# Early groups loaded a group ahead, tables on another queue, 29 units ahead of the gate matrix

## The reference

```
p  = x @ w_in                                    # q, k, v of mixers A and B, two gates
yA = attention over own chunk + 8 previous, relative-position bias per head
yB = windowed grouped attention, ALiBi penalty, a learned sink per head
h  = LN1(a*x + (sig(gA)*(yA@w_a) + sig(gB)*(yB@w_b)) @ w_out)
q  = h @ w_query  -> 8 heads x 2 halves; s1 = q1 . sub_keys_1; s2 = q2 . sub_keys_2
v1,i1 = top16(s1); v2,i2 = top16(s2); sc,ci = top16(v1 + v2)   # 16 experts per head
gate = softmax(sc); experts = e1*128 + e2        # of 128*128 experts
y  = LN2(a*h + sum over experts of gate * gelu(u[expert].h) * v[expert])
```

## Time and profile before

| | |
|---|---|
| median of 3 runs | 4519.07 us (4515.66 to 4525.55) |
| the profiled execution | 4518.42 us, span 4516.6 us |
| busy: PE, PEld, DVE, ACT, POOL | 90%, 87%, 62%, 37%, 66% of the span |
| mean granted TensorE clock | 0.947 of full speed |
| DMA | 1341.35 MB, mean 297 GB/s |

### The profile page before, as it was taken

One profiled execution on the slowest core, in us unless ns is written; L12 is line 12 of the kernel. 1 busy time (PEld: TensorE's weight loads), 2 busy tenths in 40 slices (PEclk: granted clock), 3 DMA queues, 4 the chain that ended last, 5 costly groups with the idle time before them and its releaser, 6 DMA issues. The chain is left out here.

```text
span 4516.6 us, 71733 instructions
## 1 busy us (share of the span) xinstructions
PE 4082.8 (90%) x26789; PEld 3927.0 (87%) x26789; DVE 2798.5 (62%) x4041; ACT 1666.0 (37%) x2837; POOL 2982.2 (66%) x1624
## 2 busy tenths in 40 slices
PE   7999999999998998997999789899999998787867
PEld 7988889999977877996999788899999998787867
DVE  2112322377566788875987677666776676767775
ACT  3433444443233444323335455433333333222223
POOL 6843457675754554774567466698888887676754
PEclk8988999999999998998999899999999999898989
DMA  8755446554998898995358799999999999898973
GB/s 257 226 162 154 129 140 206 160 171 139 418 359 343 344 365 327 399 389 203 117 163 318 274 325 336 336 406 416 417 416 415 415 416 385 340 379 320 383 306 102
DMA packets 366152, 1341.35 MB, mean 297 GB/s; under 512 B 35968, under 2 KB 148480, under 8 KB 280448
## 3 DMA queue, kind: packets, MB, share of 16 engines
q0 software_dynamic: 93760, 682.66, 37.2%
q1 hardware_dynamic: 141696, 510.20, 33.0%
q10 hardware_dynamic: 130496, 145.99, 9.3%
HBM read 1277.73 MB, written 65.80 MB: 297 GB/s over the span
## 5 line engine op out<-in xcount | busy, mean ns | idle before, releaser
L480 POOL TENSOR_TENSOR w_lo<-w_raw,w_hi 128x1024 fp32r<-128x1024 f32 x968 | 2345.3, 2425 | 1192.1 <-ACT w_hi L942 1170.1
L942 ACT ACTIVATE w_hi<-w_raw 128x1024 fp32r<-128x1024 f32 x968 | 1018.6, 1056 | 1315.0 <-DMA w_raw<-in_wstream 636.0
L1461 DVE CUSTOM_DVE_ANT_0 rows<-rows,banks 128x2048 f32<-128x2048 f32 x320 | 728.4, 2281 | 285.3 <-DMA rows<-in_u_rows,idx_all 284.5
L1464 DVE SCALAR_TENSOR_TENSOR banks<-rows,act_n,banks 128x2048 f32<-128x2048 f32 x320 | 752.2, 2350 | 211.9 <-DMA rows<-in_v_rows,idx_all 208.9
L879 PE MATMUL banks<-weighted,w_hi 128*128 128x320 f32 x3072 | 699.8, 317 | 92.7 <-DVE work L1856 66.8
L824 PE MATMUL banks<-mv_hi,w_hi 128*128 128x320 f32 x2048 | 654.1, 319 | 91.2 <-ACT work L1308 54.7
L545 PE MATMUL banks<-mv,w_hi 128*128 128x256 f32 x3648 | 697.9, 293 | 35.3 <-POOL w_lo L480 27.9
L545 PE MATMUL banks<-mv_hi,w_hi 128*128 128x384 f32 x1824 | 635.4, 348 | 49.6 <-ACTq L1196 21.5
L824 PE MATMUL banks<-mv_lo,w_hi 128*128 128x320 f32 x2048 | 641.9, 313 | 0.0
L824 PE MATMUL banks<-mv_hi,w_lo 128*128 128x320 f32 x2048 | 641.8, 313 | 0.0
L545 PEld LDWEIGHTS banks<-mv,w_hi 128*128 128x128 f32 x3648 | 593.3, 200 | 45.4 <-issue 28.3
(11 more groups left out here) (179 smaller groups left out, 5430.2 us busy)
## 6 DMA issues: line engine op xcount, KB each, us to landing
w_raw<-in_wstream SPq DMA_DIRECT2D x968, 512.0 KB, 5.6
gate_matrix<-work ACTq DMA_DIRECT2D x20, 1024.0 KB
work<-gate_matrix ACTq DMA_DIRECT2D x16, 1280.0 KB, 10.8
early_act<-work ACTq DMA_DIRECT2D x64, 160.0 KB, 6.1
work<-early_act ACTq DMA_DIRECT2D x64, 160.0 KB
out_p<-work ACTq DMA_DIRECT2D x34, 192.0 KB, 3.6
gate_scratch<-work ACTq DMA_DIRECT2D x32, 192.0 KB, 7.4
work<-gate_scratch ACTq DMA_DIRECT2D x16, 384.0 KB, 10.6
```

The costliest lines, as they stand in the source:

```text
L480: pool.tensor_tensor(w_lo[s][:, part], raw[s][:, part], w_hi[s][:, part].bitcast(f32), ALU.subtract) \
L942: act.activation(w_hi[s][:, HALVES[h]], raw[s][:, HALVES[h]], ACT.Copy).then_inc(hi_late, 1)
L1461: ins = dve.tensor_tensor_reduce(rows, rows, nat, 1.0, 0.0, ALU.mult, ALU.add, weight)
L1464: ins = dve.scalar_tensor_tensor(nat, rows, weight, nat, ALU.mult, ALU.add)
```

## The change

Five parts. `TAIL` goes from 19 to 29, so 35 units run beside the gate matrix and `QUAD_STEPS` becomes 7. `RATES` changes for four ranges. In the gate loop ScalarE calls `gate_rows(q + 2)` after the unit events. The tables are issued by SP, one after each unit of units 2 to 15 (the constants in four parts, 14 DMAs in all), for which the qkv loop is written out. And the early groups' gates and activations get two buffers each with a semaphore per buffer (`early_in`), `load_early(i)` issues both together, one group earlier than before; regular groups keep `G4`.

```
@@ -22,6 +22,7 @@
 SCALE = HD ** -0.5
 NEG = -1e30
 BIG = 3e38
+TABLES = 6 + 8
 PICKS = PH * TOPK
 
 G3 = 64
@@ -35,7 +36,7 @@
 GBLK = ND // GT
 GATE_Q = ND // 4
 AHEAD = 4
-TAIL = 19
+TAIL = 29
 GATE_UNITS = N_EARLY - TAIL
 QUAD_STEPS = GATE_UNITS * KT_N // GATE_Q
 ROWS = 4
@@ -84,8 +85,8 @@
         ITEMS.append(("h", _b, 0))
 FIRST_OF = {(z, b): ITEMS.index((z, b, 0)) for z, b, p in ITEMS if p == 0}
 GATHER_AT = AT["b4"] + 12
-RATES = ((GATHER_AT, AT_GATE[1], 2.3), (AT_GATE[1] + 1, AT_PROJ[1], 4.2), (AT_PROJ[1], AT_OUT[1], 2.2),
-         (AT_OUT[1], AT_QUERY[1], 2.0), (AT_EARLY + GEXP_AT, AT_EARLY + TAIL, 1.9), (AT_EARLY + TAIL, AT_LATE, 1.6))
+RATES = ((GATHER_AT, AT_GATE[1], 2.3), (AT_GATE[1] + 1, AT_PROJ[1], 4.2), (AT_PROJ[1], AT_OUT[1], 2.4),
+         (AT_OUT[1], AT_QUERY[1], 2.2), (AT_EARLY + GEXP_AT, AT_EARLY + TAIL, 2.2), (AT_EARLY + TAIL, AT_LATE, 1.2))
 
 
 
@@ -374,7 +375,8 @@
         sq_l = [W2[:, 6080 + ND * s:6080 + ND * s + ND] for s in range(2)]
         g_buf = [R[:, 5120 + 2048 * w:5120 + 2048 * w + 2048].rearrange("p (e t) -> p e t", t=GT) for w in range(2)]
         G4 = R[:, 5120:5120 + EG * ND].rearrange("p (b e t) -> p b e t", b=GBLK, e=EG)
-        act_in_t = [R[:, 7680 + ND * e:7680 + ND * e + ND] for e in range(EG)]
+        act_in_t = [[a[:, at + ND * e:at + ND * e + ND] for e in range(EG)] for a, at in ((R, 7680), (x_raw, 3072))]
+        G4_early = [a[:, 0:EG * ND].rearrange("p (b e t) -> p b e t", b=GBLK, e=EG) for a in (W2[:, 5632:], R[:, 5120:])]
 
         banks = ctx.enter_context(nc.psum_tensor("banks", [P, 8, 512], f32))
         nat = banks[:, 4:8, :].rearrange("p b c -> p (b c)")
@@ -426,7 +428,6 @@
         oh_ready, oh_gated, g_full, g_evac = sem("oh_ready"), sem("oh_gated"), sem("g_full"), sem("g_evac")
         g_stored = [sem(f"g_stored{w}") for w in range(2)]
         act_stored = [sem(f"act_stored{s}") for s in range(2)]
-        act_in = sem("act_in")
 
         rows_in = [sem(f"rows_in{s}") for s in range(ROWS)]
         rows_used, nat_ready, act_n_ready, act_n_gelu = (
@@ -434,6 +435,7 @@
         hb_taken, hb_stored, n_var, n_std, n_ready, n_stored, half_copied, acc_high = (
             sem(n) for n in ("hb_taken", "hb_stored", "n_var", "n_std", "n_ready", "n_stored", "half_copied", "acc_high"))
 
+        early_in = [sem(f"early_in{z}") for z in range(2)]
         g4_in, gelu_done, w_prod, wwh_done, w_ready, out_evac = (
             sem(n) for n in ("g4_in", "gelu_done", "w_prod", "wwh_done", "w_ready", "out_evac"))
         dve_own, dve_apart, pool_apart = sem("dve_own"), sem("dve_apart"), sem("pool_apart")
@@ -453,8 +455,33 @@
                     sp.wait_ge(mv_in[1], 16)
                 for h in range(2):
                     sp.dma_start(raw[s][:, HALVES[h]], wstream[:, s, HALVES[h]]).then_inc(raw_half[s][h], 16)
+
+            def table(dst, src):
+                sp.dma_start(dst, src).then_inc(tab_done, 16)
+
+            def bias_table(n):
+
+                rt, n_r = rext.tensor, rext.shape[1]
+                if n == 0:
+                    table(bp_a[:, 64:P, :], bass.AP(rt, 63, [[n_r, 16], [-1, 64], [1, 512]]))
+                elif n == 1:
+                    table(bp_a[:, 0:64, 0:448], bass.AP(rt, 127, [[n_r, 16], [-1, 64], [1, 448]]))
+                elif n < 6:
+                    h = slice(4 * n - 8, 4 * n - 4)
+                    table(bp_a[h, 0:64, 448:512], negs[h])
+                elif n < TABLES:
+                    b = DEC_T * (n - 6)
+                    table(bs_a[:, b:b + DEC_T, :], bass.AP(rt, 383, [[n_r, 16], [-1, 16], [1, 144]]))
+
             for name, unit, count in SEGMENTS:
-                first = 1 if name == "qkv" else 0
+                if name == "qkv":
+                    for i in range(1, count // 2):
+                        for s in range(2):
+                            for h in range(2):
+                                load(2 * i + (AT[name] + s), 2 * i + (unit + s), s, h)
+                            bias_table(2 * i - 2 + s)
+                    continue
+                first = 0
                 if count == 2:
                     for s in range(2):
                         for h in range(2):
@@ -1221,12 +1248,6 @@
                 load(subkt[:, :], subk, const_in)
                 load(sinkt[:, :], sinks, const_in)
                 load(lnt[:, :], lnp, const_in)
-                rt, n_r = rext.tensor, rext.shape[1]
-                load(bp_a[:, 64:P, :], bass.AP(rt, 63, [[n_r, 16], [-1, 64], [1, 512]]), tab_done)
-                load(bp_a[:, 0:64, 0:448], bass.AP(rt, 127, [[n_r, 16], [-1, 64], [1, 448]]), tab_done)
-                load(bp_a[:, 0:64, 448:512], negs, tab_done)
-                for b in range(DEC_B):
-                    load(bs_a[:, DEC_T * b:DEC_T * b + DEC_T, :], bass.AP(rt, 383, [[n_r, 16], [-1, 16], [1, 144]]), tab_done)
 
             for i in range(N_QKV):
                 if i == 2:
@@ -1234,7 +1255,7 @@
                 if i == 6:
                     load_constants()
                 if i == 26:
-                    act.wait_ge(tab_done, 16 * (3 + DEC_B))
+                    act.wait_ge(tab_done, 16 * TABLES)
                     first_loads(0)
                 qkv_slot(AT["qkv"] + i, i, 0)
                 if 4 <= i < 4 + KT_N:
@@ -1357,27 +1378,27 @@
                     act.wait_ge(g_stored[w], 16 * (blk // 2))
                 act.activation(g_buf[w][:, :, 4 * qq:4 * qq + 4],
                                banks[:, 2 + q % 2, :].rearrange("p (t e) -> p e t", t=4), ACT.Copy).then_inc(g_evac, 1)
-                if q + 2 < GATE_Q:
-                    gate_rows(q + 2)
                 for u, h in quad_events(q):
                     if h == 0:
                         split_high(AT_EARLY + TAIL + u + 2, 0)
                     else:
                         early_activation(TAIL + u)
+                if q + 2 < GATE_Q:
+                    gate_rows(q + 2)
                 if qq == 3:
                     act.wait_ge(g_evac, q + 1)
                     act.dma_start(G_s[:, :, blk, :, :].rearrange("g p e t -> p g (e t)"),
                                   g_buf[w].rearrange("p (g e) t -> p g (e t)", e=EG)).then_inc(g_stored[w], 16)
 
 
-            def load_gates(q):
-
-                g = (q + EARLY) % GROUPS
-                load(G4.rearrange("p b e t -> p (b e t)"), G_s[g].rearrange("p b e t -> p (b e t)"), g4_in)
-
-            def load_acts(i):
+            def load_gates(r):
+
+                load(G4.rearrange("p b e t -> p (b e t)"), G_s[EARLY + r].rearrange("p b e t -> p (b e t)"), g4_in)
+
+            def load_early(i):
+                load(G4_early[i % 2].rearrange("p b e t -> p (b e t)"), G_s[i].rearrange("p b e t -> p (b e t)"), early_in[i % 2])
                 for e in range(EG):
-                    load(act_in_t[e], a_s[EG * i + e], act_in)
+                    load(act_in_t[i % 2][e], a_s[EG * i + e], early_in[i % 2])
 
             def high_part(z, q, e, src):
                 act.wait_ge(w_prod, EG * q + e + 1)
@@ -1402,15 +1423,16 @@
                 i = q + 1 - REGULAR
                 if 0 <= i < EARLY:
                     for e in PREP[v]:
-                        high_part(1 - i % 2, q + 1, e, act_in_t[e])
+                        high_part(1 - i % 2, q + 1, e, act_in_t[i % 2][e])
                 split_high(n + 2, 1)
-                if v == 0 and q + 1 < GROUPS:
-                    act.wait_ge(w_prod, EG * (q + 1))
-                    load_gates(q + 1)
-                    if 0 <= i < EARLY:
-                        if i:
-                            act.wait_ge(w_ready, EG * (q + 1))
-                        load_acts(i)
+                if v == 0:
+                    if q + 1 < REGULAR:
+                        act.wait_ge(w_prod, EG * (q + 1))
+                        load_gates(q + 1)
+                    nxt = q + 2 - REGULAR
+                    if 0 <= nxt < EARLY:
+                        act.wait_ge(w_ready, EG * (q + 1))
+                        load_early(nxt)
 
             for w in range(2):
                 act.wait_ge(g_stored[w], 16 * (GBLK // 2))
@@ -1821,10 +1843,10 @@
 
             dve.sem_inc(out_evac, 4)
 
-            def product(act, e):
+            def product(act, gates, e):
 
                 a3 = act.rearrange("p (b t) -> p b t", b=GBLK)
-                dve.tensor_tensor(a3, a3, G4[:, :, e, :], ALU.mult).then_inc(w_prod, 1)
+                dve.tensor_tensor(a3, a3, gates[:, :, e, :], ALU.mult).then_inc(w_prod, 1)
 
             def low_part(z, q, e, src):
                 dve.wait_ge(wwh_done, EG * q + e + 1)
@@ -1847,7 +1869,7 @@
                 if e == 0:
                     dve.wait_ge(g4_in, 16 * r + 16)
                 dve.wait_ge(gelu_done, N_EARLY + EG * r + e + 1)
-                product(bank_of(e), e)
+                product(bank_of(e), G4, e)
                 if e == EG - 1:
                     low_part(0, r, e, bank_of(e))
 
@@ -1866,12 +1888,11 @@
                 i = q + 1 - REGULAR
```

(32 more changed lines are left out.)

43 lines of the change are left out of this document (21 added, 22 removed).

## The result

The changed kernel takes 4362.2 us (median; 4356.1 to 4363.4, 4 runs), the kernel before 4520.0 us beside it (4515.7 to 4525.6): ratio 0.9639, 95% interval 0.9624 to 0.9655. The gain is 158 us; 86 were forecast (4432 us). The profiled execution spans 4361.4 us, before 4516.6; the mean granted clock is 0.966, before 0.947.

The account below looks back on a forecast made before the run. Bytes were taken to pace the full-DMA stages, with the tables, gate matrix and early groups not full. Terms: 68 - 15 + 24 + 9 = 86 us off 4518.4, so 4432 us; range 4358 to 4474.

Parts of the forecast that it names:

- rival (c): Whole kernel: tables 15, projections 8 lost, units and gate matrix 60, early groups 83; 150 us gained, 4368 us; chance 0.20.
- 24 forecast: Early units and gate matrix: 108 + 153 + 340 + 4 = 605 us against 629, gain 24; ends +74 and -3.
- Three engines within 7% of each other never overlap wholly: Gate matrix with 35 units: TensorE 312, DMA 303, VectorE 291 us, so 340 taken, between 329 and 367.
- Rival (d): Gate matrix: each quad paced by its own chain, not its GEMM; 144 us more than forecast, 4576 us; chance 0.05.
- not added: Gate matrix: ScalarE serving units first removes TensorE's 54.7 us gelu wait, most of it already inside the 24 us.
- 68 forecast: Early groups loaded a group ahead: 537 us becomes 469, between DMA floors of 453 and 478; ends 83 and 45.
- rival (b): Early groups: VectorE paces them at 72 us a group, gain 33 instead of 68, 4467 us; chance 0.15.
- (e): Early groups: loading ahead brings nothing, seven periods of 76.7 us again, 4500 us; chance 0.07.
- The first wait ... nothing: Early groups' wait at 3846: its 2.6 MB only move one group forward into a full stage, so no gain.
- -15 forecast: Two projections: 3 more gathers in each, 3.15 MB at full DMA, 15.8 us; 15 lost, ends 0 and 16.
- 9 forecast: Tables on SP's queue: TensorE's 15.2 us wait goes, 6.3 us exposed, gain 9; ends 15 and -8.
- The half of 12.5 us that was to stay exposed: Tables on SP's queue: the large two cost 12.5 us of landing time, 6.3 of it taken as exposed.

Follow-up runs that it names:

- both edits taken back: Changed kernel with TAIL 19, the old rates and ScalarE's old order back, loads ahead and tables kept: 4423.6 us, ratio 0.9744 to the kernel before.
- the runs that take the six steps out: Changed kernel, projections at 2.2 and 2.0 gather steps per unit: steps to attention 4380.8 us, to units 14-28 4372.3; TAIL 19 4367.2, with old order too 4423.6.
- 3.8 steps: Changed kernel with 3.8 gather steps per unit beside the second half's attention instead of 4.2: 4378.5 us, ratio 0.9679 to the kernel before.

## Why the prediction was right or wrong

The time fell 70 us below the forecast, inside the range, and within 6 us of rival (c), "everything closes", 4368 us. Most of the mechanisms were the forecast's; three terms were mis-sized. By the table the kernel gained 69 us more than the sum: 45 in the early units and the gate matrix, 26 in the early groups and 12 by the tables, less 12 in the regular groups and 2 before the early units.

**Early units and gate matrix: 24 forecast, 69 measured.** The step that failed is "Three engines within 7% of each other never overlap wholly", with which 340 us were taken between 329 and 367 although TensorE's own floor was 312. The upper end was also worked out wrong: without the norm's 60 us the old stage has TensorE at 382 of 426 us, not of 450, so 0.90 and 348 us. And the old stage's share of TensorE, 0.86 over all of it, was no general loss of overlap. It was for the most part one coupling, the 174.4 and 54.7 us of the earlier trace rows: ScalarE held the gelu behind a late one-hot row. That was seen, and called "most of" the 24. With the coupling gone TensorE runs at 0.98, and the stage (first mask to last early gelu, 2502.0 to 2825.0) takes 323 us, 17 less than taken. Units 14 to 28, forecast at 153 us (131 by bytes and a hole of 22 for the norm), took about 132: DMA was idle in 8% of 140 us, 11 us, and only 3% from 2380 on, so most of the hole overlapped with gathers. The rest, some 10 us, is the passage from the last early to the first regular gelu, which the forecast did not price: 19.7 us before, 9.4 after; it is 19.0 with both edits taken back, 9.7 to 10.7 with one, and 9.4 to 13.6 in kernels with both and the same deal. (24 + 17 + 21 + 10 = 72, 3 too many: 2 are the 6 us from unit 28's gelu to the first mask, for which 4 were taken, and 1 is the old stage's end, 2890 for 2888.5.) Rival (d), 5.3 us or more per quad, was wrong: 323 / 80 = 4.0.

**The order, "not added" to the 24.** Right in effect, for a reason that the forecast did not have: beside 29 units it is worth nothing, and alone 51 us. One cure for one coupling was enough.

**Early groups: 68 forecast, 94 in the last stretch less some 7 to 8 in the regular groups.** For the period of 66 to 68 us the forecast was right: 65.8, DMA at 1.01, VectorE at 352 of 395 us, so not rival (b) at 72, nor (e) at 76.7. Six periods give 57.8 of the 93.8 us. The mis-sized part is the end. The forecast let seven periods shrink by one measure, DMA's floor, and gave the last group nothing. But from the last gate load on DMA is at 0.65, no floor: there the waits removed (33.8 us before, two of up to 17.1) come back whole, 246.7 - 211.1 = 35.6 us; TensorE's clock rose there too, from 0.87 to 0.94. "The first wait ... nothing" was too kind: 2.6 MB moved into a full stage cost what they cost everywhere, 2.6 / 0.41 = 6.3 us, and the regular gelus took 7.3 us more with this part alone and 7.7 less without it. The rest of their 12.4 us lies in the spread: in kernels with the same number of gathers there they took 907.4 to 912.5 us with the loads ahead, and 900.1 to 904.8 without, but 912.6 in the one with the order alone, which is left open.

The 358 GB/s of the Trainium skill ("DMA: Bandwidth & Descriptors", section "Where 436 GB/s comes from") did not bind here either: the changed kernel's trace has 410 GB/s, held for 395 us by weights, gathers, gates and activations together.

**Projections: -15 forecast, -12.8 measured**, 9.7 us per unit of the first as forecast (145.6 / 15); the runs that take the six steps out give 10.6 to 14.7 back. By bytes, as worked out. The 3.7 us of the attention before them, which no part of the change touches, lie within its spread (522.4 to 534.0 us in kernels with the same deal).

**Tables: 9 forecast, 22 alone and 18 in company.** The stretch of 57 to 80 us, called not full, was full: DMA 1.00 in the earlier trace rows. The half of 12.5 us that was to stay exposed is not seen: DMA is at 0.86 from 57 to 80 us where it was 1.00, TensorE fully busy there. The 14 DMAs lie between weights that are two units ahead, and TensorE's waits up to 100 us name none of them. The term that failed is the 6.3 us taken as exposed. The ends given, -8 to 15, did not hold the gain. TensorE's first 130 us, before and after:

```profile
0.00:130.00 130.00, 98.70 (x768) 98.06 (x769) 36.28 (x31) 51.40 (x79) 85.25 (x39) 0.91 0.79 250
0.00:130.00 130.00, 115.24 (x912) 114.24 (x913) 49.01 (x34) 60.40 (x91) 98.50 (x45) 1.00 0.85 277
```

It is ahead by 144 matmuls, which at 169 in 20 us (from 130 us on) are some 17 us: the 15.2 of the wait, and the rest by the clock, which stood at 0.83 from 57 to 80 us before and at 1.00 after. The other 4 of the 20.9 us come later, in a front whose length is not fixed (last section).

**The range.** The chance of 0.20 for (c) kept its low end near enough, by 4 us: that the time fell inside was luck as much as sizing. (The early groups' lower end was 45; by its own 70 us a period it is 537 - 490 = 47.) What the two larger errors have in common: a stage's old shares were carried into the new stage as limits, where a wait of the old one had made them.

## What to carry to other kernels

When a stage stands at 0.85 of its floor, look for the one in-order engine whose early wait holds another engine's work behind it, before calling the rest imperfect overlap; if it is found, size the stage by the floor. Two edits that each cure the same coupling don't add: test by taking each back and then both. And price a removed stall by what binds just behind it, stretch by stretch: where the DMA is full it is worth only the share that bytes leave, at the end, where nothing is full, all of it.

## What was not expected of the hardware

**One DMA, two prices of issue.** The 256 KB of `negs` took ScalarE 8.07 us to issue behind two large tables and 7.62 in the kernel with the tables put back; in four parts, one between the weights of two units, SP needed 0.60 to 0.74 us for a part, 2.6 in all. The constants of the same size, issued by ScalarE 3.4 us before, took 0.42 us (timeline of the kernel before), so size alone doesn't make it; whether the queue ahead, the shape or the engine does, no run separates.

**Equal code, two fronts.** With the tables on SP's queue the first gate eviction of the second part comes at 1217 to 1220 us in six profiles, at 1228 to 1231 in five and at 1224 in two. With them on ScalarE's it comes at 1239.7 to 1242.3 in five. In some kernels the parting is seen at 170 to 190 us, where TensorE stands idle once for under 2 us. The changed kernel and the one with the loads taken back:

```profile
170.00:190.00 20.00, 18.40 (x154) 18.23 (x154) 0.44 (x2) 7.13 (x10) 12.54 (x6) 1.00 0.91 285
```

```profile
170.00:190.00 20.00, 18.05 (x151) 17.88 (x150) 0.44 (x2) 6.83 (x9) 12.19 (x6) 1.00 0.86 283
```

and the one with both gate edits taken back:

```profile
170.00:190.00 20.00, 18.11 (x139) 17.93 (x138) 0.44 (x2) 6.65 (x9) 12.24 (x6) 0.91 0.89 284
```

The pause is as long, but a mean of 0.91 means 1.2 GHz for 3.6 of the 20 us, and 12 to 15 matmuls fewer. What decides it after pauses of 1.6 to 1.95 us these runs don't show, and it is not the whole story: of the five late fronts three have 0.91 in this stretch, and two (the 29 units taken back, and 3.8 steps) have 1.00 like the early ones. With all of it the tables are worth 20 to 25 us up to that eviction in one pair of profiles and 9 to 15 in another.

**A gather has a price by its place**: 1.6 us less for each one taken from beside the attention, 3.1 to 4.4 more for each one added, 2.4 in the regular and last stages, 2.5 to 2.8 in units 14 to 28 ((146.8 - 131.7) / 6 and (146.8 - 130.3) / 6), near the 2.6 by bytes. The deal of the changed kernel stands near the bend, as far as the moved norm lets one say.
